# Key weights and first modulation block issued by ScalarE at the head of its program, the block in eight transfers

## What is computed

```python
shift_m, scale_m, gate_m, shift_f, scale_f, gate_f = split6(silu(c) @ w_ada + b_ada)   # c: 9 rows, w_ada: 1024 x 6144
h = rmsnorm(x, g_norm_mix) * (1.0 + scale_m) + shift_m
p = h @ w_in
k_nope = einsum('tc,chd->thd', c_kv, w_uk)       # keys of 8 x 1024 cached rows: pages of 128 rows
k = rmsnorm(concat([k_nope, k_rope]), g_qk_k)    # needs the sum of squares of each key and head
x = x + gate_m * (merged_branches @ w_out)
x = x + gate_f * moe(h2)                         # 64 experts, top 8
```

## Time and profile before

| | |
|---|---|
| median of 3 runs | 986.41 us (985.37 to 986.9) |
| the profiled execution's own time | 987.81 us |
| its span | 986.0 us |
| busy: TensorE, VectorE, ScalarE, GpSimd | 956.5, 565.7, 207.2, 101.5 us |
| moved by DMA | 311.89 MB, 316 GB/s on the mean |
| granted TensorE clock, mean | 0.998 |

### The profile page before, as it was taken

One profiled execution on the slowest core, in us unless ns is written; L12 is line 12 of the kernel. 1 busy time (PEld: TensorE's weight loads), 2 busy tenths in 40 slices (PEclk: granted clock), 3 DMA queues, 4 the chain that ended last, 5 costly groups with the idle time before them and its releaser, 6 DMA issues.

```text
span 986.0 us, 14540 instructions
## 1 busy us (share of the span) xinstructions
PE 956.5 (97%) x4985; PEld 532.3 (54%) x4985; DVE 565.7 (57%) x1412; ACT 207.2 (21%) x418; POOL 101.5 (10%) x76
## 2 busy tenths in 40 slices
PE   6999999999999999999999999999999999999997
PEld 2487766544546778888753443443443444444343
DVE  2613322468764011123746888787877788878774
ACT  3321231335435100002411111111111111111111
POOL 0000010100000000000111122122112112211100
PEclk9999999999999999999999999999999999999999
DMA  8995469755546375535589999999999999999992
GB/s 311 418 409 214 179 203 312 221 156 171 166 129 261 129 316 228 213 128 209 220 295 416 424 421 437 424 422 430 431 420 432 426 425 421 431 426 429 428 422 96
DMA packets 49643, 311.89 MB, mean 316 GB/s; under 512 B 8538, under 2 KB 28026, under 8 KB 32818
## 3 DMA queue, kind: packets, MB, share of 16 engines
q1 hardware_dynamic: 43378, 297.28, 75.6%
q0 software_dynamic: 5904, 12.79, 3.7%
q10 hardware_dynamic: 304, 1.08, 0.3%
HBM read 315.80 MB, written 3.95 MB: 324 GB/s over the span
## 4 chain that ended last, share of the span: by engine, by line
PE 76%; DMA 13%; SPq 5%; DVE 3%; issue 2%; ACT 0%; DVEq 0%; ACTq 0%
PE bank L816 45%; PE pA L816 19%; DMA ring<-in_w_e_gu 12%; PE pB L816 5%; PE pC L816 4%; SPq L467 3%; PE pD L816 2%; SPq L511 1%; SPq L506 1%; DMA pT<-in_poolT 1%; PE pA L1377 0%; PE pA L849 0%; DMA ring<-in_poolT 0%; DVE xT L2437 0%; DVE hT L2310 0%
## 5 line engine op out<-in xcount | busy, mean ns | idle before, releaser
L816 PE MATMUL pA<-ring,qT 128*64 128x512 f32 x976 | 226.8, 595 | 8.3 <-DMA ring<-in_w_e_gu 8.2
L2420 DVE STREAM_TRANSPOSE qT<-xs 32x256 f32<-32x256 f32 x480 | 209.2, 436 | 7.6
L816 PE MATMUL bank<-hT,ring 128*128 128x264 f32 (+1 forms) x832 | 191.5, 390 | 2.3 <-ACTq L1688 2.3
L816 PEld LDWEIGHTS bank<-hT,ring 128*128 128x128 f32 (+1 forms) x832 | 155.2, 190 | 36.4 <-issue 9.9
L816 PEld LDWEIGHTS pA<-ring,qT 128*64 128x64 f32 x976 | 71.7, 137 | 136.7 <-issue 127.6
L788 POOL DMA_INDIRECT xs<-h_rows,idx x32 | 79.5, 2485 | 372.9 <-DVE idx L2400 276.8
L816 PE MATMUL bank<-wuk,ring 128*128 128x512 f32 x192 | 86.3, 597 | 0.0
L816 PE MATMUL bank<-pT 128*128 128x256 bf16 (+1 forms) x500 | 85.6, 273 | 0.0
L816 PE MATMUL bank<-pT,vtok 128*128 128x256 bf16 (+1 forms) x264 | 71.8, 281 | 0.0
L816 PE MATMUL pB<-ring,oaT 128*64 128x512 f32 x240 | 62.0, 605 | 0.0
L816 PE MATMUL pC<-ring,oaT 128*64 128x512 f32 x240 | 60.3, 592 | 0.0
(11 more groups left out here) (357 smaller groups left out, 941.5 us busy)
## 6 DMA issues: line engine op xcount, KB each, us to landing
ring<-in_w_e_gu SPq DMA_DIRECT2D x27, 4096.0 KB, 19.7
ring<-in_w_e_dn SPq DMA_DIRECT2D x34, 1024.0 KB, 15.6
ring<-in_w_e_dn SPq DMA_DIRECT2D x13, 2048.0 KB, 17.7
ring<-in_w_e_gu SPq DMA_DIRECT2D x7, 2048.0 KB, 9.9
ring<-in_poolT SPq DMA_DIRECT2D x64, 208.0 KB, 2.7
ring<-in_w_ada SPq DMA_DIRECT2D x12, 1024.0 KB, 10.5
ring<-in_w_bg SPq DMA_DIRECT2D x4, 3072.0 KB, 11.6
ring<-in_w_mix SPq DMA_DIRECT2D x5, 2048.0 KB, 8.8
```

What stands on the lines that cost most here:

```text
L816: return nc.tensor.matmul(out, lhsT, rhs, start=start, stop=stop)
L2420: last = V.transpose(xTs[32 * j:32 * j + 32, q % 2, :, 32 * a:32 * a + 32], src[32 * a:32 * a + 32, j])
```

## The change

SyncE no longer issues `wuk` nor block 0. ScalarE issues `wuk` as the first instruction of its program, and after its sigmoid block 0 in eight transfers, one for each 128 rows of the block's 1024, each of 128 rows of 2 KB (256 KB). All of it lands at the same places and is counted by the same semaphores; block 0 now adds 8 x 16 to `wgt[0]`, so `ITEMS` gives it eight transfers, and all later readers of slot 0 wait for values that are higher by 112. Nothing is computed in another way, and no other order changes.

```diff
--- before.py
+++ after.py
@@ -86,7 +86,7 @@
 
 
 PAGES = [("pages", NPG)] * 4
-ITEMS = [[(n, 1) for n in ("ada0", "in0", "ch")] + PAGES
+ITEMS = [[("ada0", 8)] + [(n, 1) for n in ("in0", "ch")] + PAGES
          + [("g1", 1), ("g3", 1), ("exp", 1)],
          [(n, 1) for n in ("ada1", "cb", "u")] + PAGES
          + [("g2", 1), ("exp", 1)],
@@ -473,11 +473,9 @@
                                  .rearrange("o p c -> (o p) c")).then_inc(d_early[g], 16)
 
             sp.dma_start(ptab[:], A["ptab"]).then_inc(d_ptab, 16)
-            sp.dma_start(wuk, A["w_uk"]).then_inc(d_early[0], 16)
             sp.wait_ge(d_ptab, 16)
             early_pages(0)
             early_pages(1)
-            ada_item(0)
             sp.dma_start(xT[:], A["xT"]).then_inc(d_in, 16)
             sp.dma_start(vec[:], A["vec"]).then_inc(d_in, 16)
             early_pages(2)
@@ -1530,9 +1528,12 @@
                 act.wait_ge(full[b], k + 1)
                 return bk[b]
 
+            act.dma_start(wuk, A["w_uk"]).then_inc(d_early[0], 16)
             act.wait_ge(d_c, 16)
             act.wait_ge(s["consts"], 1)
             nc.scalar.activation(csig[:, :, 0:NC], cT[:], ACT.Sigmoid).then_inc(s["csig"], 1)
+            for k in range(DT):
+                act.dma_start(part(0, 0, DT, 512)[:, k], A["w_ada"][0][:, k]).then_inc(wgt[0], 16)
 
             def early_squares(e0, e1):
                 for e in range(e0, e1):
```

## The result

The changed kernel is slower. Its median is 991.0 us over 7 runs (989.15 to 992.23) against 986.65 us for the kernel before on the same chip; the ratio is 1.0044, with a 95% interval of 1.0032 to 1.0055. The forecast was 984.7, with 986.4 as the upper end. The profiled execution has a span of 990.3 us, against 986.0.

A forecast was written before the change was run, and what follows sets the result against it. TensorE's start was taken as bound by late data, first by issue, then by bytes. The norm chain's -1.86 and the first page's +0.1 gave -1.76 on 986.41: 984.65, predicted as 984.7 us, range 983.7 to 986.4.

The forecast's parts named there:

- Step (1): Kernel start, key weights moved to ScalarE: first page's issue gains 0, its transfer gets 0.2 us back.
- Step (3): First pages sharing DMA engines with block 0: 0.3 us taken, bounds 0 and 0.64; first page 0.1 us later.
- Step (4): Block 0 lands at 13.4 to 15.2 us; TensorE's idle 1.16 and 1.63 us before block and key 4 close.
- Step (5): VectorE's norm chain is late next: it comes 1.86 us earlier, so 0.9 of TensorE's 2.79 us is given back.
- (C): At the start, pages wait behind block 0, TensorE pauses, matmuls run slow: +4.7 us, 991.1, with twelve slow; chance 0.07.
- (A): Block 0 still comes last, at 15.7 us, its 2 KB rows losing against xT's 8 KB rows: 985.7 us; chance 0.13.
- (D): ScalarE's table load precedes the key weights' issue, adding 0.1 to 0.3 us: 984.9 us; chance included in the forecast's 0.62.
- (B): At the start only SyncE's issue time, 0.47 us, is saved; pages and xT are held up: 985.9 us; chance 0.12.

The follow-up runs named there:

- e2: Changed kernel with the key weights back on SyncE, so only block 0 goes to ScalarE; 988.97 us, ratio 1.0015.
- e10: Kernel before, with the page table issued first and only page 3 issued by ScalarE, after its sigmoid; 985.16 us, ratio 0.9985.
- e1: Kernel before, with only the key weights moved to the head of ScalarE; 988.81 us, ratio 1.0018.
- e3: Changed kernel, with the key weights in two transfers of 2 KB rows instead of one of 4 KB rows; 990.05 us, ratio 1.0038.
- e7: Changed kernel, with the page table issued ahead of the conditioning vectors; 988.7 us, ratio 1.0021.
- e8: Kernel before, with the page table first and pages 1 and 3 issued by ScalarE after its sigmoid; 991.27 us, ratio 1.0058.
- e11: e10 with the key weights issued by SyncE directly behind the page table, ahead of the conditioning vectors; 988.7 us, ratio 1.0017.
- e5: e2 with block 0 held back until the key weights and first page have landed; 990.19 us, ratio 1.0034.
- e9: e8 with ScalarE issuing its two pages ahead of its sigmoid; 986.16 us, ratio 0.9995.
- e4: e2 with block 0 in one transfer of 16 KB rows instead of eight transfers; 992.02 us, ratio 1.0058.

## Why the prediction was wrong

**What bounds the kernel** was right: the first page, the block and the norm chain, and a shift that is handed on, though not one for one: the fold of the changed kernel is 5.04 us late and its span 4.3, that of e2 4.63 and 2.8. e10 has the sign that was forecast, with another change.

**Step (1), "0 is gained at the issue", failed.** The 0.35 us that SyncE saves is nothing, as said; but nothing was asked of what the key weights, issued at 0.83 by the other engine, do to cT and the table, issued at 0.83 and 1.30. The table was 2.33 us later for the first page (5.79 against 3.46). e1 shows it alone: +2.2 us of time. In the prediction wuk was only "no longer ahead of p0"; it was in fact now ahead of the table that p0 waits for.

**Step (3), the price of sharing, failed by its upper bound.** The bound was one whole transfer, 0.64 us. Page 0 took 6.52 instead of 2.4, so +4.1 us, and the pages of e2 4.0 to 6.2. The bound counted one turn; the runs show packets that come late and then take turns many times, one for each row of the page on an engine. cosT's 5.8 us was the row nearest to it: as an addition of 5.8 - 2.2 = 3.6 us it lay close to the 4.1 measured, though no run shows that its mechanism is the same, and it was set aside because "here the large ones are 2 KB". The span from 0.64 to 3.6 us should have stood in the range.

**Step (4)** was right in what it said of the idle times (1.16 and 1.63 us both closed), but for a poor reason: TensorE was so late that all had landed. The block itself came no earlier. In the changed kernel its last part, issued near 7.5 and 8.0 us on its way, landed near 15.5, as the whole block did before (15.55); in e2, issued near 6.3 and 10.0 us on its way, near 16.3. Both are after the 13.4 to 15.2 of the sum. For the half-empty window of 4.6 to 9.0 us, the changed kernel shows 232 GB/s against 179, and e2, whose block is issued from 2.75 on, 292, not the 350 that were expected: moving the issue did not fill it.

```profile
4.60:9.00 4.40, 0.00 (x0) 0.00 (x0) 0.21 (x1) 0.00 (x0) 0.00 (x0) 1.00 0.77 232
```

**Step (5), the norm chain, was right**: VectorE's four sums of keys run one behind the other (2.46 us), and the fold waits for VectorE 1.45 us.

```profile
30.27 2.46 DVE L1911 TENSOR_REDUCE kss_e<-qT 128x8 f32<-128x512 f32 x4 [0.15 <-DVE rstd L1916]
```

The sum for the fold then works: +6.47 for the start, +0.68 as keys 0 to 3 take 9.31 us instead of 8.63 (the matmuls four and five are slow, 0.85 and 0.90 us instead of 0.59 and 0.42), -1.16 - 1.63 for the idle times, +0.72 for VectorE: +5.08, measured +5.04.

**The rivals.** (C) gave +4.7 us, and +4.35 was measured, but that is by chance. Pages behind the block are the second half of what happened. Its other half, matmuls at the lower level behind a pause, did not happen in the changed kernel, whose wait lay before the first matmul; slow matmuls cost it 0.7 us more than before. In e2, e3, e7, e8 and e11, where a pause came after key 0, four to seven of the twelve matmuls were slow: this half was real, with n below the 12 that gave +4.7. (A) was real, seen in e5: the block landed at 20.2. (D) did not happen: the key weights went out at 0.83, ahead of the table load. (B) gave 985.9, and so had the wrong sign like the forecast; it was nearer only in size. The Trainium skill (DMA: Bandwidth & Descriptors, Issuing engines are not separate DMA queues) states its rule, that transfers of several issuing engines interleave on the same DMA engines and that only the sequencer's time is saved. The interleaving is in the traces, 136 packets beside 127 from 12 to 13 us; a time saved in the whole is not, for the change cost 4.35 us.

## What to carry to other kernels

In this kernel a transfer issued on another engine was not simply beside the first queue. So ask of each small transfer on which others wait (a table, a first page) what both engines issue shortly before it, keep large ones behind, and not only just behind (e11). e10 is the pattern that worked here: the second engine issues one small transfer of the same urgency, and the large ones follow from the queue that issued the other small ones. Count a pause of TensorE near its start with more than its length: behind 1.7 us came 3.0 us of slow matmuls in e2, and 0.1 in e5. Where the only row for a shared resource is far away and several times the estimate, keep it as the end of the range.

## What the runs showed of the hardware

A transfer of 128 KB on one queue took 2.0 to 2.1 us with nothing ahead (e1), and its first packet ran 1.0 us after the issue. Issued within some microseconds after the first transfer of a large block by the other engine, it took 4.0 to 9.0 us (the changed kernel, e2 to e5, e7, e8). For part of that time its queue shows next to no packets, though they would have been running without the block: 0 beside 163 from 7 to 8 us in the changed kernel, 2 beside 150 in e2, 2 beside 48 in e8. Issued before it, it took 2.4 (e7, by 0.07 us), 2.7 (e9) and 2.4 us (e10), but 7.2 in e11. So the late packets go with the order of issue over both engines, in both directions (e8 against e9, and page 1 against page 2 in e7). What the stage is that makes them late can't be read from these traces, and no run held the order and changed only the distance in time.

Where both queues had packets throughout, they ran one for one whatever their size: 136 to 127 with 2 KB and 1 KB, 63 to 60 with 8 KB and 2 KB (e5), 26 to 24 with 16 KB and 1 KB (e4). Between the two states are windows such as 133 to 36.

The time of one execution also holds a piece that the start doesn't set. In all kernels TensorE waits 2.3 us near 355 to 361 us. In nine of the fourteen profiled executions the 32 matmuls behind it then take about 9.0 us, in five 7.36; over 340 to 380 us the granted clock (third value from the right) is 0.96 in the profiled execution of before, the first row, and 1.00 in that of e2, the second:

```profile
340.00:380.00 40.00, 37.73 (x189) 31.73 (x188) 4.33 (x10) 3.36 (x11) 0.00 (x0) 0.96 0.80 326
```

```profile
340.00:380.00 40.00, 37.72 (x198) 31.78 (x197) 5.13 (x14) 3.45 (x11) 0.00 (x0) 1.00 0.82 334
```

That is 1.7 us, as much as many of the differences here, and one reason why a single span can't be compared (e2's fold is 4.6 us late and its span ends only 2.8 us late). In executions of one kernel the clock goes with the time too: the changed kernel's two with a mean granted clock of 1.000 took 989.15 and 989.43 us, its other five, at 0.997 to 0.999, 990.8 to 992.2. The five profiled executions without the dip, e2, e3, e7, e8 and e11, are just those with four or more slow matmuls behind a pause at key 1. Why the two go together stays open. So does how many slow matmuls the other executions of e2 had: its fold of +4.6 us, of one execution, holds 3.4 us by them and by a slower key 0, and its median of +2.4 may hold less; no run was made for it.
